# One more tile, another layout of the powers and another schedule for the S5 matrices in an MLA / S5 / ConvFFN encoder

## What is computed

```python
for i in range(DEPTH):                      # DEPTH = 2
    hn = rmsnorm(h, g_mix[i])
    mix = mla_mixer(hn, ...) if i % 2 == 0 else s5_mixer(hn, ...)
    h = h + mix
    h = h + conv_ffn(rmsnorm(h, g_ffn[i]), w_up[i], conv_w[i], conv_b[i], w_down[i])
return rmsnorm(h, g_final)

def conv_ffn(h, w_up, conv_w, conv_b, w_down):
    val, gate = split(causal_depthwise_conv3(h @ w_up, conv_w) + conv_b)   # 2 x 2816 wide
    return (silu(gate) * val) @ w_down

# s5: 64 groups of 16 channels with 64 complex states each
# x_t = a * x_(t-1) + bbar u_t;   y_t = Re(c x_t) + d u_t;   gelu(y) @ w_glu, gated
```

## Time and profile before

| what | before |
|---|---|
| median of 3 runs | 1181.65 us (1181.65 to 1187.68) |
| profiled execution | 1180.64 us |
| its span, first to last instruction | 1178.6 us |
| TensorE busy | 1124.9 us (95%) |
| VectorE busy | 811.3 us (69%) |
| ScalarE busy | 456.1 us (39%) |
| GpSimd busy | 127.9 us (11%) |
| mean granted TensorE clock | 0.985 |

### The profile page before, as it was taken

The page is one execution under the profiler, slowest core; times in us unless marked ns, Lnnn a source line. Parts: engine busy times, 40 slices in busy tenths (PEclk is TensorE's granted clock), DMA queues, the critical chain, the costliest instruction groups (busy, mean ns, idle before and its releaser), DMA issues.

```text
span 1178.6 us, 14622 instructions
## 1 busy us (share of the span) xinstructions
PE 1124.9 (95%) x5596; PEld 912.2 (77%) x5596; DVE 811.3 (69%) x1151; ACT 456.1 (39%) x677; POOL 127.9 (11%) x222
## 2 busy tenths in 40 slices
PE   5899999999999999989999999999999999999995
PEld 4777558788888887868777887887888888888874
DVE  6786655798886888658875884555775367635764
ACT  5422553454522553216452233334443244423441
POOL 3837107900000000000000000000000000000000
PEclk9999999999999999989999989999999999999998
DMA  6222002233333333423345883323232232233221
GB/s 218 74 97 90 1 1 72 72 102 113 104 133 103 126 125 107 126 72 111 108 157 167 238 239 89 112 92 102 90 105 92 94 103 90 90 107 101 87 81 71
DMA packets 61749, 125.60 MB, mean 107 GB/s; under 512 B 21744, under 2 KB 30320, under 8 KB 61680
## 3 DMA queue, kind: packets, MB, share of 16 engines
q1 hardware_dynamic: 60528, 120.48, 32.4%
q0 software_dynamic: 1152, 4.19, 1.1%
HBM read 109.97 MB, written 14.68 MB: 106 GB/s over the span
## 4 chain that ended last, share of the span: by engine, by line
PE 69%; DVE 19%; issue 3%; ACT 3%; DVEq 2%; DMA 2%; SPq 1%; ACTq 0%
PE bank L1168 22%; PE bank L1170 21%; PE bank L1169 21%; DVE WL L659 4%; DVE CV L914 2%; DVE Z L904 1%; DVE MX L777 1%; ACT CV L586 1%; DVE CV L911 1%; PE bank L1383 1%; DVE HH L893 1%; DVE SS L670 1%; DMA ud_scratch<-UB 1%; DVEq L913 1%; DVE Pexp L785 1%
## 5 line engine op out<-in xcount | busy, mean ns | idle before, releaser
L426 ACT ACTIVATE WH<-RAW 128x1024 fp32r<-128x1024 f32 (+1 forms) x184 | 190.0, 1033 | 412.5 <-PE bank L1170 374.5
L1168 PE MATMUL bank<-GH,WH 128*128 128x512 f32 x816 | 323.7, 397 | 19.1 <-DVE GL L697 12.7
L1170 PE MATMUL bank<-GH,WL 128*128 128x512 f32 x816 | 319.1, 391 | 0.0
L1169 PE MATMUL bank<-GL,WH 128*128 128x512 f32 x816 | 319.1, 391 | 0.0
L659 DVE TENSOR_TENSOR WL<-RAW,WH 128x1024 fp32r<-128x1024 f32 (+1 forms) x184 | 221.7, 1205 | 39.9 <-ACT WH L426 39.5
L1168 PE MATMUL bank<-AH,WH 128*128 128x512 f32 x596 | 236.9, 398 | 6.9 <-DVE AL L897 5.8
L1170 PE MATMUL bank<-AH,WL 128*128 128x512 f32 x596 | 233.9, 392 | 0.0
L1169 PE MATMUL bank<-AL,WH 128*128 128x512 f32 x596 | 233.8, 392 | 0.0
L1168 PEld LDWEIGHTS bank<-GH,WH 128*128 128x128 f32 x816 | 154.2, 189 | 54.9 <-issue 13.9
L1169 PEld LDWEIGHTS bank<-GL,WH 128*128 128x128 f32 x816 | 154.2, 189 | 32.6 <-issue 1.2
L1170 PEld LDWEIGHTS bank<-GH,WL 128*128 128x128 f32 x816 | 154.0, 189 | 32.7
(11 more groups left out here) (228 smaller groups left out, 991.2 us busy)
## 6 DMA issues: line engine op xcount, KB each, us to landing
RAW<-in_w_up SPq DMA_DIRECT2D x88, 512.0 KB, 3.5
RAW<-in_w_dn SPq DMA_DIRECT2D x32, 512.0 KB, 3.5
RAW<-in_w_glu SPq DMA_DIRECT2D x16, 512.0 KB, 3.6
RAW<-in_w_dn SPq DMA_DIRECT2D x16, 384.0 KB, 3.0
RAW<-in_w_wo SPq DMA_DIRECT2D x8, 512.0 KB, 3.6
od_scratch<-OO SPq DMA_DIRECT2D x8, 512.0 KB, 3.3
kd_scratch<-KT SPq DMA_DIRECT2D x8, 512.0 KB, 5.0
RAW<-in_w_win SPq DMA_DIRECT2D x8, 512.0 KB, 4.7
```

Of the source, the lines that this page charges most:

```text
L426: act_(WH[b % RH][:, :n], RAW[b % RW][:, :n], ACT.Copy).then_inc(s_hi, 1)
L1168: mm(out, wh, hi_[:, k, :], start=start, stop=False)
L1169: mm(out, wh, lo_[:, k, :], start=False, stop=False)
L1170: return mm(out, wl, hi_[:, k, :], start=False, stop=stop)
```

## The change

The S5 matrix operations start in wo (one per block) in place of up00; in the last two blocks of each up phase there are none; dn00 and dn01 keep three per block, and dn02 has one per block while any are left. TensorE's `matrices` come three blocks after a group's last operation throughout. There are two O tiles, used in turn: OO0 stays where OO was, OO1 lies over PA and PB, so the first write to it waits for `s_wcs`; from group 2 on the first write waits for the group two before. The powers are laid out `[P, NQ, LQ + 1]`. VectorE's loop for wo is moved behind the definition of `matrix_op`, and calls `matrices_of(b)` at its end.

```diff
-FFN0 = range(FIRST["up00"], FIRST["win"])
+FFN0 = range(FIRST["wo"], FIRST["win"])
...
-    _up = PHASE_OF[_b].startswith("up") or PHASE_OF[_b] == "dn02"
-    OPS_AT[_b] = range(_i, min(_i + (1 if _up else 3), MAT_OPS * NJ))
+    _p = PHASE_OF[_b]
+    _ops = 3 if _p in ("dn00", "dn01") else 0 if _p.startswith("up") and FIRST[_p] + BLOCKS[_p] - _b <= 2 else 1
+    OPS_AT[_b] = range(_i, min(_i + _ops, MAT_OPS * NJ))
...
-            _n = _b + (2 if PHASE_OF[_b] == "dn02" else 3)
+            _n = max(_b + 3, FIRST["up00"])
...
+        pa_at = at
         PA, at = place("PA", [P, 512], F32, at)
         PB, at = place("PB", [P, 512], F32, at)
-        OO, at = place("OO", [P, 2, QJ, C, LQ], F32, at)
+        OO = [None, place("OO1", [P, 2, QJ, C, LQ], F32, pa_at)[0]]
+        OO[0], at = place("OO0", [P, 2, QJ, C, LQ], F32, at)
...
-        PWR, at = place("PWR", [P, LQ + 1, NQ], F32, at)
-        PWI, at = place("PWI", [P, LQ + 1, NQ], F32, at)
+        PWR, at = place("PWR", [P, NQ, LQ + 1], F32, at)
+        PWI, at = place("PWI", [P, NQ, LQ + 1], F32, at)
...
-                    pr, pi = (t[:, 1:LQ + 1, qs] for t in (PWR, PWI))
+                    pr, pi = (t[:, qs, 1:LQ + 1] for t in (PWR, PWI))
...
-                    pr, pi = (t[:, LQ - 1::-1, qs] for t in (PWR, PWI))
+                    pr, pi = (t[:, qs, LQ - 1::-1] for t in (PWR, PWI))
...
-                pr, pi = (x.rearrange("p m q -> p q m").unsqueeze(2).broadcast_to(sh) for x in (pr, pi))
+                pr, pi = (x.unsqueeze(2).broadcast_to(sh) for x in (pr, pi))
...
-                    if j >= 1:
-                        dve.wait_ge(s_et, j)
-                        dve.wait_ge(s_ow, 16 * j)
-                    v.tensor_tensor(OO[:, 0], TA[:], TB[:], ALU.add)
+                    if j == 1:
+                        dve.wait_ge(s_wcs, 1)
+                    if j >= 2:
+                        dve.wait_ge(s_et, j - 1)
+                        dve.wait_ge(s_ow, 16 * (j - 1))
+                    v.tensor_tensor(OO[j % 2][:, 0], TA[:], TB[:], ALU.add)
...
+            for j, b in enumerate(span("wo")):
+                dve.wait_ge(s_mm, b + 1)
+                add_x(b, j)
+                lo(b + RH)
+                next_tile("n_wo", "ffn0", j, first=(j == 0))
+                matrices_of(b)
...
-            g.memset(PWR[:, 0, :], 1.0)
-            g.memset(PWI[:, 0, :], 0.0)
+            g.memset(PWR[:, :, 0], 1.0)
+            g.memset(PWI[:, :, 0], 0.0)
             g.drain()
             for k in range(LQ):
-                m = cmul(PWR[:, k + 1, :], PWI[:, k + 1, :], PWR[:, k, :], PWI[:, k, :], f["ar"], f["ai"],
+                m = cmul(PWR[:, :, k + 1], PWI[:, :, k + 1], PWR[:, :, k], PWI[:, :, k], f["ar"], f["ai"],
                          f["t1"], f["t2"])
```

More of the change, by code:

```diff
@@ L352, in spill @@
                 sp.wait_ge(s_O, j + 1)
-                sp.dma_start(OD[j], OO[:].rearrange("p r q c s -> p r (q c s)")).then_inc(s_ow, 16)
+                sp.dma_start(OD[j], OO[j % 2][:].rearrange("p r q c s -> p r (q c s)")).then_inc(s_ow, 16)
             def lags(j):
@@ L813, in add_x @@
                 v.tensor_tensor(X[:, j, :], bank[BANK[b]][:], X[:, j, :], ALU.add).then_inc(s_ev, 1)
[L815 to L819, removed]
             def matrix_op(i):
@@ L853, in matrix_op @@
                     v.drain()
-                    v.tensor_tensor(OO[:, 1], TA[:], TB[:], ALU.subtract).then_inc(s_O, 1)
+                    v.tensor_tensor(OO[j % 2][:, 1], TA[:], TB[:], ALU.subtract).then_inc(s_O, 1)
                 elif o == 6:
@@ L1325, in matrices @@
                     for q in range(QJ):
-                        mm(bank[6][32 * q:32 * q + 32, 0:P], BBK[:, r, q, :], OO[:, r, q].rearrange("p c s -> p (c s)"),
+                        mm(bank[6][32 * q:32 * q + 32, 0:P], BBK[:, r, q, :], OO[j % 2][:, r, q].rearrange("p c s -> p (c s)"),
                            start=(r == 0), stop=(r == 1), skip_group_check=True)
```

## The result

| | before | after |
|---|---|---|
| median of the runs (4 each) | 1183.39 us | 1171.16 us |
| profiled execution | 1180.64 us | 1168.75 us |
| span | 1178.6 us | 1167.0 us |
| VectorE busy | 811.3 us | 795.4 us |

A forecast was written before the change was run, and what follows sets the result against it. TensorE, busy 1124.9 of 1178.6 us, was taken as the bound. From 1180.64 profiled, 14.8 gained, 2.4 and 0.1 lost gave 1168.3; 1.0 more gave the median 1169.3 us, range 1165.5 to 1174.0.

The forecast's parts named there:

- the stretch: Between output projection and S5 projection: TensorE loses 15.75 us to late VectorE, of which 14.8 us is gained.
- the projection: Output projection: eight added VectorE operations, slowed by GpSimd beside them, make TensorE wait, costing 2.4 us.
- a wait near block 30: Ahead of block 30, the first matrices come with about 3 us left; 0.1 us charged for it.
- The four waits go, and 7.1 us with them: Two O tiles: VectorE's four waits to write OO vanish, with TensorE's 7.1 us loss at up02 number 2.
- The 7.7 us that the prediction gave to the pause: Ahead of dn00, dn01 and dn02: VectorE arrives level, gaining 0.65 + 3.75 + 4.25 - 0.95 us.
- (b): Rival: the powers are no faster, up pairs stay at 10.7 to 10.9 us; 1171.9 us, chance 0.10.
- the walk: Output projection, block by block: VectorE's lateness from charged operations less idle time, reaching 2.4 us at block 6.
- the upper bound: Output projection: each new operation 1.3 us longer, a whole wide GpSimd operation; 5.5 us, before any clock drop.
- (d): Rival: the stall moves to a wait the layout missed, taking 6 us and more; 1175 to 1182, chance 0.06.
- (e): Rival: slower, contention in the output projection eats all the gain; 1189.8 at 4.5 us per operation, chance 0.02.
- (a): Rival: the output projection costs 4 to 8 us by full blocking or a clock drop; 1172.9, chance 0.14.
- (c): Rival: the output projection costs nearly nothing (0.7 us), or S5 gains a little; 1167.3, chance 0.18.

The follow-up runs named there:

- t_only: Kernel before the change with two O tiles alone, old schedule and old powers; ratio to the kernel before 0.9933.
- s_only: Kernel before the change with the new schedule alone, old powers and one O tile; ratio to the kernel before 0.9915.
- one_tile: Changed kernel with one O tile and the old waits; ratio to the kernel before 0.9869.
- table_late: Changed kernel with one O tile and GpSimd's turns table begun behind the output projection; projection 51.25 us, sums to S5 394.74 us, one run.
- old_powers: Changed kernel with the old layout of the powers; ratio to the kernel before 0.9913.
- p_only: Kernel before the change with the powers' new layout alone, old schedule and one O tile; ratio to the kernel before 0.9951.

## Why the prediction was right, and where not

- **Sum and sign.** 12.3 us forecast on the profiled time, 11.9 measured; 1169.3 forecast for the median, 1171.16 measured (range 1165.5 to 1174.0). That the sum came so close is partly luck, since its errors cancel: 2.15 us too pessimistic in the stretch and the projection (0.6, 1.45, and 0.1 for a wait near block 30 that did not come), against 2.9 in two stages that were taken at nothing (1.05 and 1.85).
- **The stretch.** 14.8 forecast, 15.4 measured. Each bracket went as said, and 0.95 ahead of dn02 stayed (0.78 in the row). Of the missing 0.6, 0.25 is in the up02 bracket: behind the transposes the next matmul starts 0.84 us after them when nothing stalls, and it came 5.60 after, so 4.76 was lost and not the 4.51 of the bracket. Another 0.2 is a miscount: from 460.02 to 464.23 there are 12 starts but 11 steps, for which 2.50 us are due, so that 1.7 was lost there and not 1.5. The last 0.15 is not traced.
- **Which part does what.** This step failed. "The four waits go, and 7.1 us with them" gave the second tile what the schedule does without it: the tile is enough with the old order (t_only), but not needed with the new one (s_only, one_tile). I had laid the new order out block by block only for two tiles. For one tile, the same list says that group 2 waits from 41 to 43, group 3 from 45 to 47, group 5 from 64 to 66 and group 6 from 68 to 70: at most two blocks, never the four that ran TensorE out of split weights. Three of these waits are in s_only's rows; group 5's is not there, and 0.64 us long in one_tile (468.30). The 7.7 us that the prediction gave to the pause, with the powers' help, came in s_only without fast powers.
- **Powers.** 692 ns right, also for the negative step (line 864, TA from PWR backwards). A pair of up blocks costs 10.06 us in after (Z at 242.23 and at 252.29), 10.2 forecast. The rule of the Trainium skill ("SBUF — State Buffer", section "The DMA port swizzle (why `[64,N]` ≈ `[32,N]`)") on 16-byte lines agrees with the 692 ns at a step of 4 bytes; of negative steps it says nothing, and here they cost nothing either. Their worth was overstated in rival (b): 2.6 us forecast without them, 1.0 measured, plus the chance of a low clock.
- **The projection.** 2.4 us forecast, 0.95 measured, and TensorE waited 1.28 us for GL and SS where the sign had been 2 to 3; the mechanism was right (table_late), the term mis-sized. VectorE's adds and some of the new operations in after:

```profile
201.73 0.68 DVE L816 TENSOR_TENSOR X<-bank,X 128x512 f32<-128x512 f32 x1
...
207.06 0.69 DVE L816 TENSOR_TENSOR X<-bank,X 128x512 f32<-128x512 f32 x1 [0.46 <-PE bank L1176]
...
211.38 1.77 DVE L673 TENSOR_TENSOR SS<-SS,SQ 128x512 f32<-128x512 f32 x1
...
213.08 1.55 DVE L850 TENSOR_TENSOR TB<-PWI,CRE 128x512 f32<-128x512 f32 x1
...
214.55 0.68 DVE L816 TENSOR_TENSOR X<-bank,X 128x512 f32<-128x512 f32 x1
...
219.07 0.69 DVE L853 TENSOR_TENSOR OO<-TA,TB 128x512 f32<-128x512 f32 x1
...
219.68 0.68 DVE L816 TENSOR_TENSOR X<-bank,X 128x512 f32<-128x512 f32 x1
220.28 1.28 DVE L662 TENSOR_TENSOR WL<-RAW,WH 128x1024 fp32r<-128x1024 f32 x1
221.48 0.74 DVE L810 SCALAR_TENSOR_TENSOR GL<-X,GAIN,GH 128x512 fp32r<-128x512 f32 x1
222.15 1.53 DVE L673 TENSOR_TENSOR SS<-SS,SQ 128x512 f32<-128x512 f32 x1
...
223.77 1.37 DVE L855 TENSOR_TENSOR TA<-PWR,BBR 128x512 f32<-128x512 f32 x1
...
225.06 0.68 DVE L816 TENSOR_TENSOR X<-bank,X 128x512 f32<-128x512 f32 x1
```

  The first add of the projection starts 1.06 us later than before, so how late VectorE is at an add is its start, less its start in the earlier trace rows, less 1.06. That gives 0.1 us at 201.73, 0 at 207.06, 2.0 at 214.55, 1.7 at 219.68 and 0.94 at 225.06, where the walk had 0.1, 0, 0.9, 1.1 and 2.4. It held up to block 3, was too low for block 4 and too high for block 6. Part of the excess is the charge: the eight took 0.69, 0.95, 1.05, 0.69, 1.55, 0.69, 1.37 and 1.75, and the five of them that the walk adds up (blocks 2 to 6) 5.35 us where I had charged 6.35. Three did not grow at all, as line 853 at 219.07. The other part is VectorE's old operations, whose lengths I had carried over. They depend on what GpSimd does beside them, and the new ones move them: in block 4 the sum of squares at 211.38 took 1.77 (before 1.54), but in block 6 the weight split, GL and the sum of squares took 1.28, 0.74 and 1.53 where they had taken 1.92, 1.53 and 1.79 before, 1.7 us less. The rule of the Trainium skill ("SBUF — State Buffer", section "Who interferes with whom"), that the later of the two blocks fully, agrees in kind with the rows of 1.55, 1.75 and 1.77; the upper bound made from it (5.5 us) takes each operation as blocked, which did not happen.
- **Rivals.** (d) and (e) did not occur. (a) did not occur in after, but its clock drop did in three of the seven kernels that have the eight operations beside GpSimd (s_only, old_powers, one_tile), and in none where TensorE waited 0.63 us or less there. (b) fell with the durations. (c) was wrong in its S5 part, but its 0.7 us for the projection was nearer to the 0.95 than my 2.4.
- **What I left at nothing.** GpSimd's slower powers were "hidden by 54.8 us of idle time". They were hidden for GpSimd, and cost the attention 0.7 us in after, since they moved GpSimd's wide operations against VectorE's softmax rows. I asked who waits for GpSimd, and not whom it blocks.

## What to carry to other kernels

When an engine far from the bound stalls the bound one, first look at how far its wait is from what it waits for in program order: a schedule that brings the two together can do all that a second buffer does, as it did here. Where two engines slow each other, moving the work of one moves the contention, so cost it where it lands, for both, also when only its length changed and nobody waits for it. And cut traces into stages between marks on the bound engine: the two stages that the change touches repeated within 0.03 us, where the spans of the same kernel were 1167.0 and 1172.8.

## What the runs showed of the hardware

- With the same two waits of TensorE (0.79 and 0.49 us, 1.0 us apart), the granted clock fell to 0.50 in one kernel out of five, for 3.2 us of lost time.
- Nor does the length of one wait decide it: the clock was 0.50 behind 2.10 us at 460.02, and 1.00 behind 1.57 us in p_only (578.67), 1.99 in t_only (575.87) and 2.50 in table_late (330.77), while behind 1.86 us in table_late (259.82) it was 0.50 again (262 to 264).
- Reading backwards by 4 bytes costs VectorE nothing (692 ns for 128 x 512); reading with 128 bytes between elements costs 0.40 to 0.43 us more (1089 to 1123 ns).
- The S5 stage, with many small transfers, varied by 6.7 us (100.0 to 106.7) between kernels whose operations there are the same but for the turn of one store. The end of the attention varied by 5.0 us (176.3 to 181.3), with the clock from 40 to 50 us (0.66 to 1.00) and from 110 to 120 us (0.83 or 1.00).
